# A two-layer encoder trunk: the residual is multiplied by the mean square, the positive part stays unscaled, and three of four pairs of the second MLP matrix are crossed

## The reference

```python
def rmsnorm(x, g, eps=EPS):
    y = x * rsqrt(mean(x * x, axis=-1, keepdims=True) + eps)
    return y * g

def sq_relu_mlp(y, w_up, w_down):          # w_up 1024 x 4096, w_down 4096 x 1024
    u = y @ w_up
    return square(relu(u)) @ w_down

h = h + sq_relu_mlp(rmsnorm(h, norm_gains[i, 1]), w_up[i], w_down[i])
```

## Time and profile before

| | |
|---|---|
| median of 3 runs | 1193.12 us (1191.04 to 1195.39) |
| the profiled execution | 1191.83 us |
| its span, on the page | 1190.0 us |
| PE busy | 1176.9 us, 99% |
| DVE, ACT, POOL busy | 957.8, 739.8, 114.4 us |
| layer 0's MLP | about 251 to 601 us of the span |
| layer 1's MLP | about 843 us to the end |
| granted TensorE clock | 0.999 of full speed |

### The profile page before, as it was taken

One profiled execution on the slowest core, in us unless ns is written; L12 is line 12 of the kernel. 1 busy time (PEld: TensorE's weight loads), 2 busy tenths in 40 slices (PEclk: granted clock), 3 DMA queues, 4 the chain that ended last, 5 costly groups with the idle time before them and its releaser, 6 DMA issues.

```text
span 1190.0 us, 22842 instructions
## 1 busy us (share of the span) xinstructions
PE 1176.9 (99%) x8809; PEld 1126.6 (95%) x8809; DVE 957.8 (80%) x1423; ACT 739.8 (62%) x1305; POOL 114.4 (10%) x171
## 2 busy tenths in 40 slices
PE   9999999999999999999999999999999999999998
PEld 8999999999999999999999999987798999989988
DVE  6889888887888888877568898887878888978953
ACT  5777877745556565554357888787565655656643
POOL 3221120100110110101010000000001101001000
PEclk9999999999999999999999999999999999999999
DMA  7343342432563453573132122213434536546622
GB/s 178 96 106 92 89 102 85 140 116 72 143 144 107 107 144 107 122 223 122 54 89 72 54 71 65 85 45 114 136 104 110 142 107 152 133 124 134 193 84 72
DMA packets 152375, 131.87 MB, mean 111 GB/s; under 512 B 23209, under 2 KB 143073, under 8 KB 152289
## 3 DMA queue, kind: packets, MB, share of 16 engines
q1 hardware_dynamic: 141600, 104.93, 30.6%
q0 software_dynamic: 10560, 25.66, 9.5%
q10 hardware_dynamic: 128, 0.09, 0.0%
HBM read 111.43 MB, written 19.24 MB: 110 GB/s over the span
## 4 chain that ended last, share of the span: by engine, by line
PE 77%; issue 17%; DVE 2%; DMA 1%; ACT 1%; POOL 1%; DVEq 0%; POOLq 0%; ACTq 0%
PE ps L2327 31%; PE ps L2279 21%; PE ps L2044 18%; PE ps L2546 2%; PE ps L2099 1%; DMA raw<-in_mlp_w_up_dram 1%; PE ps L2117 1%; PE ps L2231 0%; PE ps L2196 0%; DMA meta_in<-in_meta_tokens_dram 0%; PE ps L2185 0%; DVE lo L1657 0%; ACT wh L762 0%; DVE ps L1682 0%; POOL khm L748 0%
## 5 line engine op out<-in xcount | busy, mean ns | idle before, releaser
L2044 PE MATMUL ps<-yh,wh 128*128 128x264 f32 (+1 forms) x704 | 160.5, 302 | 0.0
L2044 PE MATMUL ps<-yh,wl 128*128 128x264 f32 (+1 forms) x704 | 155.3, 295 | 0.0
L2044 PE MATMUL ps<-yl,wh 128*128 128x264 f32 (+1 forms) x704 | 155.3, 294 | 0.0
L2327 PE MATMUL ps<-th,hi 128*128 128x264 f32 (+1 forms) x448 | 127.0, 284 | 3.6 <-ACT pu L762 3.5
L762 ACT ACTIVATE hi<-lof 128x1024 fp32r<-128x1024 f32 x80 | 82.8, 1054 | 76.6 <-DVE lof L1650 76.6
L1657 DVE TENSOR_TENSOR lo<-lof,hi 128x1024 fp32r<-128x1024 f32 x80 | 97.0, 1223 | 37.5 <-ACT hi L762 37.5
L2327 PE MATMUL ps<-tl,hi 128*128 128x264 f32 (+1 forms) x448 | 126.5, 282 | 0.0
L2327 PE MATMUL ps<-th,lo 128*128 128x264 f32 (+1 forms) x448 | 126.5, 282 | 0.0
L762 ACT ACTIVATE hi<-raw 128x1024 fp32r<-128x1024 f32 (+1 forms) x128 | 115.2, 915 | 15.0 <-DMA raw<-in_mlp_w_up_dram 11.7
L2279 PE MATMUL ps<-ah,hi 128*128 128x264 f32 (+1 forms) x448 | 115.6, 316 | 0.0
L2279 PE MATMUL ps<-al,hi 128*128 128x264 f32 (+1 forms) x448 | 115.6, 316 | 0.0
(11 more groups left out here) (325 smaller groups left out, 3288.6 us busy)
## 6 DMA issues: line engine op xcount, KB each, us to landing
raw<-in_mlp_w_up_dram SPq DMA_DIRECT2D x32, 1024.0 KB, 6.6
raw<-in_mlp_w_down_dram SPq DMA_DIRECT2D x32, 1024.0 KB, 5.0
raw<-in_diff_w_in_dram SPq DMA_DIRECT2D x24, 512.0 KB, 3.8
raw<-in_mlstm_w_in_dram SPq DMA_DIRECT2D x16, 512.0 KB, 4.4
h_sum<-abuf POOLq DMA_DIRECT2D x24, 264.0 KB, 7.4
h_sum<-abuf POOLq DMA_DIRECT2D x24, 256.0 KB, 7.0
h_sum<-h POOLq DMA_DIRECT2D x16, 264.0 KB, 2.5
h<-h_sum POOLq DMA_DIRECT2D x2, 2112.0 KB, 12.8
```

Of the source, the lines that this page charges most:

```text
L2044: last = mm(ps[:, bank + s, 0:w_], w[:, slot, kb, :], m[:, kb, t0:t0 + w_], start=(kb == 0 and n == 0), stop=(kb == CB - 1 and n == 2))
L2327: last = mm(ps[:, bank, 0:w], x[1 - i % 2][:, at, :], y, start=(kb == 0 and n == 0 and name in ("A11", "S1", "A12")), stop=(kb == 3 and n ...
```

## The change

- **Scaling.** r is positive, so relu(r u)^2 = r^2 relu(u)^2, and with s = mean square + eps, h + r^2 D = (s h + D) / s. ACT now writes relu(u) without a factor (`positive`), in the place of DVE's L1726. ACT also writes s to `abuf1` (one more ACTIVATE in `norm_factor`) and 1/s to `rb` (exponent -1 in place of -1/2). DVE multiplies h by s in four instructions (`scale_residual`) ahead of the saves to `h_sum`, refines 1/s by two instructions (`refine_factor`), and in the last group writes the sum to `tbuf` and then multiplies it by 1/s (`evacuate`, `tail_sum`).
- **Transfers.** h goes to `h_sum` in 4 transfers and comes back in 4, the later ones each behind one more pair.
- **Crossed pairs.** `DOWN_FROM = 5`: the down pairs 5, 6, 7 of the first three groups are crossed. Six pairs more, three per layer. The sums of squares are made in two parts (`block_forms(..., part)`), part 0 in the iteration of the last up pair, part 1 in that of the plain pair 4; S3's low half is made in the plain pair's iteration, ahead of the forms of pair 6 (counted in the group), instead of in the first crossed pair's.

```diff
-DOWN_FROM = 6
+DOWN_FROM = 5
@@ residuals (POOL)
-                for k in range(CB):
-                    pool.wait_ge(h_ready, 16 * layer + k + 1)
-                    pool.dma_start(h_sum[k], h[:, k, :]).then_inc(h_saved, 16)
+                for q in range(4):
+                    pool.wait_ge(h_scaled, FACTOR * layer + q + 1)
+                    pool.dma_start(h_sum[2 * q:2 * q + 2, :, t0:T].rearrange("k p t -> p k t"),
+                                   h[:, 2 * q:2 * q + 2, t0:T]).then_inc(h_saved, 16)
...
-                pool.dma_start(h[:, :, :], h_sum.rearrange("k p t -> p k t")).then_inc(h_back, 16)
+                for q in range(4):
+                    if q > 0:
+                        pool.wait_ge(m_done, N_DONE * layer + DONE[PAIRS - 9 + q, "A22"])
+                    pool.dma_start(h[:, 2 * q:2 * q + 2, t0:T], h_sum[2 * q:2 * q + 2, :, t0:T].rearrange("k p t -> p k t")).then_inc(h_back, 16)
@@ norm_factor (ACT)
+                if n % 2:
+                    nc.scalar.activation(tokens(ab[1], spans), src, ACT.Identity, bias=eps_d[:, 0:1], scale=1.0 / D).then_inc(ms_rd, 1)
@@ ACT, MLP
+                def positive(i, m):
...
+                    wait(act, ah_done, 8 * (4 * layer + i // 8) + 2 * (i % 8) + m - 1)
+                    nc.scalar.activation(pair_tokens(tb[m], layer, i), pair_out(layer, i, m), ACT.Relu).then_inc(m_evac, 1)
                 def squares(i, m):
+                    if i > 0:
+                        positive(i, m)
...
+                    if i == 1:
+                        positive(0, 1)
+                        squares(0, 0)
+                        squares(0, 1)
@@ DVE, MLP
-                def block_forms(i, names):
+                def block_forms(i, names, part):
...
+                    kb = slice(2 * part, 2 * part + 2)
+                def scale_residual():
+                    dve.wait_ge(ms_rd, layer + 1)
+                    for q in range(4):
+                        rows = h[:, 2 * q:2 * q + 2, t_in:T]
+                        V.tensor_tensor(rows, rows, ab[1][:, t_in:T].unsqueeze(1).broadcast_to([P, 2, T - t_in]),
+                                        ALU.mult).then_inc(h_scaled, 1)
+                def refine_factor():
+                    made, ms, r = FACTOR * layer + 5, ab[1][:, t_in:T], rb[:, t_in:T]
+                    dve.wait_ge(rb_ready, norm + 1)
+                    V.scalar_tensor_tensor(ms, ms, -1.0, r, ALU.mult, ALU.mult).then_inc(h_scaled, 1)
+                    dve.wait_ge(h_scaled, made)
+                    V.scalar_tensor_tensor(r, ms, 2.0, r, ALU.add, ALU.mult).then_inc(h_scaled, 1)
@@ evacuate (DVE)
-                        V.scalar_tensor_tensor(pair_tokens(tb[m], layer, i), src, 0.0, pair_tokens(rb, layer, i),
-                                               ALU.max, ALU.mult).then_inc(m_evac, 1)
-                    V.tensor_tensor(tokens(h[:, k, :], spans), src, tokens(h[:, k, :], spans), ALU.add).then_inc(m_evac, 1)
+                    V.tensor_tensor(tokens(tbuf, spans), pair_out(layer, i, m), tokens(h[:, k, :], spans), ALU.add).then_inc(row_sum, 1)
+                    dve.wait_ge(row_sum, 8 * layer + k + 1)
+                    V.tensor_tensor(h[:, k, t_in:T], tbuf[:, t_in:T], rb[:, t_in:T], ALU.mult).then_inc(m_evac, 1)
@@ DVE's loop over i
                     if i == 0:
                         plain_lo(layer, 1, 0)
                         plain_lo(layer, 1, 1)
-                        evacuate(0, 0)
                         for n in range(4):
                             forms_lo(n)
+                        scale_residual()
...
+                    if i < PAIRS - 8 and i % 8 == 3:
+                        block_forms(i, ("S3", "S1", "S2", "A22"), 0)
...
+                    if sent_down(i) and i % 8 == DOWN_FROM - 1:
+                        block_lo(i + 1, "S3")
@@ tail_sum (DVE)
-                V.tensor_tensor(h[:, k, cols], ps[:, j % 2, 0:XH], h[:, k, cols], ALU.add).then_inc(m_evac, 1)
+                V.tensor_tensor(tbuf[:, cols], ps[:, j % 2, 0:XH], h[:, k, cols], ALU.add).then_inc(row_sum, 1)
+                dve.wait_ge(row_sum, tail_count(12, part, j))
+                V.tensor_tensor(h[:, k, cols], tbuf[:, cols], rb[:, cols], ALU.mult).then_inc(m_evac, 1)
```

More of the change, by code:

```diff
@@ L1041, in snap @@
                         copy(pu[:, 1, 0:w], product_bank(layer, i, "S2")).then_inc(p_copied, 1)
+                def positive(i, m):
+                    if not crossed(i):
+                        act.wait_ge(m_done, items + DONE[i, m])
+                    else:
+                        if m == 1:
+                            act.wait_ge(m_done, items + DONE[i, "A22"])
+                        act.wait_ge(c_done, adds + ADDED[i, "C22" if m else "C1"])
+                    wait(act, ah_done, 8 * (4 * layer + i // 8) + 2 * (i % 8) + m - 1)
+                    nc.scalar.activation(pair_tokens(tb[m], layer, i), pair_out(layer, i, m), ACT.Relu).then_inc(m_evac, 1)
                 def squares(i, m):
@@ L1133, in mlp @@
                         form_hi(i + 1, "S23")
-                    if i > 0 and not in_tail(layer, i - 1) and not sent_down(i - 1) and not (sent_down(i) and i % 8 == 4) and not begins:
+                    if i == 1:
+                        positive(0, 1)
+                        squares(0, 0)
+                        squares(0, 1)
+                    elif i > 0 and not in_tail(layer, i - 1) and not sent_down(i - 1) and not (sent_down(i) and i % 8 == 4) and not begins:
                         finish(i - 1, 1)
@@ L1146, in mlp @@
                             split_unit(U_IN1, 0, 1, 0)
-                        finish(i, 0)
+                        if i == 0:
+                            positive(0, 0)
+                        else:
+                            finish(i, 0)
                     if i + 2 < PAIRS:
@@ L1634, in mlp @@
                 items, ranks, norm = layer * N_DONE, layer * N_CROSSED, 2 * layer + 1
-                copies, adds = layer * N_COPIED, layer * N_ADDED
+                copies, adds, t_in = layer * N_COPIED, layer * N_ADDED, spans[0][0]
                 def form(i, name, after):
@@ L1765, in mlp @@
                         act_lo(i - 1, 1)
-                        block_forms(i, ("S3", "S1", "S2"))
-                    if begins and not is_up(i):
-                        block_lo(i, "S3")
+                        block_forms(i, ("S3", "S1", "S2"), 1)
                     if crossed(i + 1):
@@ L1800, in mlp @@
                         plain_lo(layer, i + 1, 1)
+                    if sent_down(i) and i % 8 == DOWN_FROM - 1:
+                        block_lo(i + 1, "S3")
                     if layer == 0 and i == PAIRS - 1:
                         split(U_IN1, 0)
-                    if is_up(i) and not crossed(i):
-                        if i > 0:
-                            evacuate(i, 0)
+                    if i == PLAIN:
+                        refine_factor()
+                    if i == 1:
+                        act_lo(0, 0)
+                        act_lo(0, 1)
+                    if is_up(i) and not crossed(i) and i > 0:
                         act_lo(i, 0)
-                        evacuate(i, 1)
                     elif not is_up(i) and not in_tail(layer, i) and not sent_down(i):
```

49 lines of the change are left out of this document (19 added, 30 removed).

## The result

| | before | changed |
|---|---|---|
| median | 1193.48 us (1191.04 to 1195.39) | 1212.85 us (1212.68 to 1214.49) |
| the profiled execution | 1191.83 us | 1212.68 us |
| its span | 1190.0 us | 1210.7 us |
| mean granted TensorE clock | 0.999 | 0.995 |

The ratio is 1.0172, with a 95% interval of 1.0159 to 1.0185. I had forecast 1212 and a range of 1197 to 1219.

What follows compares the result with a forecast made beforehand. PE was taken to bound the kernel, as long as DVE and ACT deliver in time. 1191.8 - 7.7 - 2.8 + 8.4 + 21.4 + 0.5 = 1211.6, forecast as 1212 us, range 1197 to 1219.

Steps and rivals of the forecast that it cites:

- What bounds: Whole kernel: PE, busy 99% of the span, sets the time as long as DVE and ACT deliver in time.
- the steady run: Successive crossed up pairs: DVE needs 10.1 us against PE's 10.26, fits barely, so 0.
- Crossed pairs, -7.7: Three more crossed pairs per layer: each saves PE 1.43 us in layer 0, 1.14 in layer 1; -7.7 us.
- Transfer, -2.8: Transfer back to h in four parts: the slow weight load at 521.46 and PE's wait behind it go; -2.8 us.
- Starts, +8.4: Start of each MLP: multiplications of h by s make PE wait, 4.6 us in layer 0, +3.8 in layer 1.
- its third part: Layer 0's start, after two longer waits: PE waits 0.55 us for P5 and 0.8 for P1 of pair 3.
- First crossed down pair, +21.4: Six groups: DVE's chain comes late for PE; +10.0 us in layer 0, +11.4 in layer 1.
- the second wait: In each of six groups, at the pair after the first crossed down pair: PE idle 1.4 us, ended by `pu`.
- The rest, +0.5: Last group's added multiplication per block: hidden beside PE except a 256-wide one in the tail; +0.5 us.
- Fewer matmuls alone: Rival: no wait at the MLP starts or first crossed down pairs, 1181.8 us; chance 0.04.
- covered: Rival: waits at the MLP starts, none at the crossed down pairs; 1190 us, no change; chance 0.05.
- Half of it: Rival: starts pass without the loop over `al`, each group loses only the first 1.95 us; 1197 to 1200; chance 0.13.

Runs made afterwards that it cites:

- the last run: The changed kernel with two crossed down pairs per group and S3's low half back in the crossed pair: 1199.97 us, ratio 1.0062.
- the run with the forms first: The changed kernel with pair 6's four formed halves ahead of its plain low half, before each group's first crossed down pair: 1205.58 us, ratio 1.0109.

## Why the forecast was right, and where not

- **What bounds.** PE, as long as DVE delivers: right. The test is the last run, in which the groups run at PE's own pace although ACT has the positive parts (nothing lost in the steady run, as forecast), and the run with the forms first, where 1.1 us of DVE's chain came back as 1.1 us of time.
- **Crossed pairs, -7.7.** Right: a group of layer 0 is -1.43 plus its two waits, as worked out above; the closeness of 0.02 us is in part chance.
- **Transfer, -2.8.** Right: +1.69 in two groups and -1.12 in the third differ by 2.8; alone it brings 2.4 us in the third group, and 0.33% of the time (3.9 us) by its ratio, whose interval reaches down to 2.4.
- **Starts, +8.4.** 9.7 measured. Layer 0: 1.5 + 2.05 + 1.5 less 0.1 for 4.6; its third part was forecast as waits (1.35) and came as a slower clock, under which PE had nothing to wait for. That the two come out alike is chance in part: in the run with the forms first the clock stayed up at this place, and pairs 2 and 3 took 24.03 us, for 24.17. Layer 1: PE stands 2.03, 2.04, 0.35 and 1.09 us for 1.7, 1.6, 0.55 and 0.9; the first two were too small by my steps.
- **First crossed down pair, +21.4.** 1.92 and 1.19 us in layer 0 for 1.95 and 1.4. All that the groups lost, from the table with PE's saving and the transfer's put back: 2.3 + 4.3 + 2.8 = 9.4 in layer 0 (forecast 10.0), 6.7 + 3.4 = 10.1 in layer 1 (forecast 11.4). DVE's chain came 0.2 us sooner than forecast (C22 at 23.6 and not 23.85), and as the step behind it, from C22 to the product S2, is 4.42 us for 4.43, the second wait is shorter by that. In the third group of each layer the second wait never came: behind the first one TensorE went at 1.2 GHz (granted clock 0.50 from 498.14 and from 1092.06 on), which cost 1.5 us in its place. The forecast has no clock in it, and that this loss and the wait are of like size is chance.
- **The rest, +0.5.** The term that was mis-sized: 2.6. I wrote "hidden beside PE except the last" of a multiplication behind each sum, by the length of the instruction and PE's share of the time. I had not looked whether DVE and ACT wait for each other there. They do, and the run without the multiplication gives 2.6 us of the span back.
- **The sum is closer than its parts.** Starts and end were 3.4 us too small, the groups 1.9 too large, the program up to the MLP 0.5 shorter: 1.0 in all, which is 1211.6 against the profiled 1212.7.
- **Two slips of arithmetic.** 7.6 + 1.2 + 1.20 is 10.0 and not 10.1 for a crossed up pair, and 276.7 - 275.49 is 1.21 and not 1.25 for the first wait (1.50 measured). Neither moves the forecast.
- **The rivals.** "Fewer matmuls alone" and "covered" fell with the waits at both places. "Half of it" was not so far off as a kernel: it is what stands when part 0 comes in time (1201.8). Relu on ScalarE, which a rule of the Trainium skill (ScalarE: Activation LUTs, Rules for kernel authors) advises against, with VectorE's speed in bf16 as the reason, took 602 ns from PSUM for 128x528 float32 (L1061), DVE's former instruction 704: for float32 from PSUM the rule is not borne out here, as the sum had it.

Open stays what is best for the second wait of each group, for P1 behind C1 and ACT's `send` (0.9 to 1.2 us in the rows of the versions with three crossed pairs); no run took it away.

## What to carry to other kernels

- A step can only be taken out from under a busy engine if the engines that feed it are ahead at that place. Write down their queue in order with durations from the event that starts it, and compare with when the consumer is due: that gave 23.9 us for 23.7.
- Where two engines wait for each other in a round, neither is full and still nothing is hidden: any instruction added to the round lengthens it. Look for brackets on both sides before you call an addition free.
- Ahead of an instruction that waits for another engine's result, put work that waits for nothing; behind it, nothing that a third engine needs. One low half on either side of four forms made 18.8 us in the kernel with two crossed pairs; in the one with three, where it stood behind the forms, PE waited 2.3 us for it in each of six groups.
